# Value projections with the tokens stationary: 512 features wide in two half-depth chunks, in place of 256 features wide in two full-depth chunks

## The reference

```python
def token_mixing(u, w_in, ...):                       # mixer 0
    proj = u @ w_in
    gq, gk, gv, glr, gog, mq, mk, mv, ga, gb = jnp.split(proj, offsets, axis=-1)   # gv, mv: 512 wide each
    o_a = gla_chunked(heads(gq), heads(gk), heads(gv), heads(log_a))
    o_b = moba_attention(heads(mq), heads(mk), heads(mv), rel_bias)
    ...
for l in range(DEPTH_2):                              # mixers 1 and 2
    x = x + 0.5 * swiglu_2(rms_norm(x, ffn1_norm[l]), ffn1_w_in[l], ffn1_w_out[l])
    h = rms_norm(x, mix_norm[l]) @ w_mix_in[l]
    (c_x, c_b, c_c, h_q, h_f, h_i, h_g, f_q, f_k, f_v, f_f) = jnp.split(h, split_at, axis=-1)   # f_v: 512 wide
```

## Time and profile before

| | |
|---|---|
| median of 3 runs | 1642.5 us (1640.9 to 1642.66) |
| the profiled execution: span | 1640.7 us |
| TensorE busy | 1616.5 us (99%), 13617 records |
| VectorE busy | 1154.1 us (70%) |
| ScalarE busy | 799.1 us (49%) |
| GpSimd busy | 171.4 us (10%) |
| TensorE clock granted | 1.000 over the span |

### The profile page before, as it was taken

How to read it: one execution, slowest core, us unless ns; L and a number is a source line. 1 busy time by engine, 2 the same in 40 slices (tenths; PEclk the granted TensorE clock), 3 DMA queues, 4 the chain that set the end, 5 groups by cost and what they waited for, 6 DMA issues and landing times.

```text
span 1640.7 us, 33817 instructions
## 1 busy us (share of the span) xinstructions
PE 1616.5 (99%) x13617; PEld 1579.3 (96%) x13617; DVE 1154.1 (70%) x1452; ACT 799.1 (49%) x973; POOL 171.4 (10%) x193
## 2 busy tenths in 40 slices
PE   6999999999999999999999999999999999999999
PEld 4999999999999999999999999999999999999999
DVE  6877789778766657666688876656665588776653
ACT  3444445355544455444565654445444465554432
POOL 1100114500000000000052200000000035200000
PEclk9999999999999999999999999999999999999999
DMA  9998897646666467665744566568665764456653
GB/s 332 303 315 250 250 329 229 221 147 189 183 190 184 135 193 203 187 169 159 231 134 129 152 179 183 154 180 217 193 181 149 204 186 129 129 162 191 170 159 114
DMA packets 501553, 315.62 MB, mean 192 GB/s; under 512 B 14815, under 2 KB 489674, under 8 KB 501450
## 3 DMA queue, kind: packets, MB, share of 16 engines
q1 hardware_dynamic: 491824, 282.33, 60.5%
q0 software_dynamic: 8496, 29.92, 5.2%
q10 hardware_dynamic: 1130, 1.90, 0.3%
HBM read 313.04 MB, written 1.05 MB: 191 GB/s over the span
## 4 chain that ended last, share of the span: by engine, by line
PE 71%; DVE 4%; ACT 2%; issue 1%; ACTq 0%; DVEq 0%
PE accs L1747 20%; PE accs L1749 20%; PE accs L1748 19%; PE wide L1787 1%; PE accs L1787 1%; PE accs L1785 1%; PE wide L1785 1%; PE accs L1786 1%; PE wide L1786 1%; DVE wlo L1060 1%; PE wide L2018 1%; PE accs L1845 1%; PE accs L1847 0%; PE accs L1846 0%; PE ps_score L2067 0%
## 5 line engine op out<-in xcount | busy, mean ns | idle before, releaser
L1747 PE MATMUL accs<-uhi_shift,whi 128*128 128x256 f32 x2304 | 650.8, 282 | 3.0 <-DVE ulo L1111 1.2
L1749 PE MATMUL accs<-uhi_shift,wlo 128*128 128x256 f32 x2304 | 645.8, 280 | 0.0
L1748 PE MATMUL accs<-ulo,whi 128*128 128x256 f32 x2304 | 643.2, 279 | 0.0
L746 ACT CAST whi<-raw 128x2048 fp32r<-128x2048 f32 (+2 forms) x294 | 499.5, 1702 | 101.4 <-PE accs L1749 61.9
L1060 DVE TENSOR_TENSOR wlo<-raw,whi 128x2048 fp32r<-128x2048 f32 (+2 forms) x249 | 496.3, 2001 | 4.5 <-ACT gat L987 3.1
L1747 PEld LDWEIGHTS accs<-uhi_shift,whi 128*128 128x128 f32 x2304 | 433.4, 188 | 11.3 <-issue 5.2
L1748 PEld LDWEIGHTS accs<-ulo,whi 128*128 128x128 f32 x2304 | 434.3, 188 | 1.2 <-issue 1.2
L1749 PEld LDWEIGHTS accs<-uhi_shift,wlo 128*128 128x128 f32 x2304 | 433.2, 188 | 0.0
L1747 PE MATMUL accs<-hhi,whi 128*128 128x256 f32 x1056 | 297.6, 282 | 0.7 <-DVE wlo L1060 0.7
L1748 PE MATMUL accs<-hlo,whi 128*128 128x256 f32 x1056 | 298.0, 282 | 0.0
L1749 PE MATMUL accs<-hhi,wlo 128*128 128x256 f32 x1056 | 296.3, 281 | 0.0
(11 more groups left out here) (368 smaller groups left out, 2258.7 us busy)
## 6 DMA issues: line engine op xcount, KB each, us to landing
raw<-in_ffn_w_in SPq DMA_DIRECT2D x176, 512.0 KB, 5.1
in_turn<-in_w_ada POOLq DMA_DIRECT2D x56, 512.0 KB, 5.5
raw<-in_w_mix_in SPq DMA_DIRECT2D x52, 512.0 KB, 4.7
raw<-in_ffn_w_out SPq DMA_DIRECT2D x64, 384.0 KB, 3.6
raw<-in_w_ff_gate SPq DMA_DIRECT2D x44, 512.0 KB, 5.0
raw<-in_w_ff_up SPq DMA_DIRECT2D x44, 512.0 KB, 6.3
raw<-in_w_in SPq DMA_DIRECT2D x40, 512.0 KB, 5.0
raw<-in_ffn_w_out SPq DMA_DIRECT2D x64, 320.0 KB, 4.0
```

What stands on the lines that cost most here:

```text
L746: nc.scalar.copy(whi[:, n % RING, 0:cols], raw[:, n % RING, 0:cols]).then_inc(hi_ready, 1)
L1747: mm(dst, wh, xh, start=first, stop=False)
L1748: mm(dst, wh, xl, start=False, stop=False)
L1749: return mm(dst, wl, xh, start=False, stop=last)
```

## The change

The value chunks become pairs of a new kind "p". Both chunks of a pair cover the same 512 output columns; the first holds row tiles 0 to 3 (input features 0 to 511), the second row tiles 4 to 7. A chunk is now 2 token blocks x 4 row tiles x 3 = 24 products of 512 columns. Token block 0 accumulates in bank e % 2 over both chunks, token block 1 in bank (e+1) % 2. So the second bank is asked for in the middle of the first chunk, token block 0 is complete in the middle of the second (new counter `token_ready`), and VectorE evacuates it in the step of the second chunk. In mixers 1 and 2 chunk `av1` moves ahead of `g4`, so that the pair is adjacent; `lv0` there stays as it was.

```diff
-GLA_CHUNKS = [("lq", 0, "f"), ("lk", 256, "f"), ("lv0", 512, "t"), ("lv1", 768, "t"),
+GLA_CHUNKS = [("lq", 0, "f"), ("lk", 256, "f"), ("lv0", 512, "p"), ("lv1", 512, "p"),
...
-              ("av0", 2576, "t"), ("av1", 2832, "t"), ("g0", 1040, "f"), ("g2", 1296, "f")] + \
+              ("av0", 2576, "p"), ("av1", 2576, "p"), ("g0", 1040, "f"), ("g2", 1296, "f")] + \
...
-              ("ak0", 2304, "f"), ("ak1", 2560, "f"), ("av0", 2816, "t"), ("g4", 0, "f"), ("av1", 3072, "t"),
+              ("ak0", 2304, "f"), ("ak1", 2560, "f"), ("av0", 2816, "p"), ("av1", 2816, "p"), ("g4", 0, "f"),
...
+            def wide_rows(w, n, at, half_):
+                v = kview(raw, n % RING, KD // 2, 512)
+                src = w[half_ * D // 2:(half_ + 1) * D // 2, at:at + 512].rearrange("(k p) c -> p k c", p=P)
+                return [(v[:, 2 * j:2 * j + 2], src[:, 2 * j:2 * j + 2]) for j in range(2)]
...
+                if kind == "p":
+                    tt = int(name[2])
+                    if tt == 0:
+                        dve.wait_ge(token_ready, m + 1 + (m > 0 or name == "av0"))
+                    else:
+                        dve.wait_ge(chunk_used, RING + n0 + s + 1)
+                    v.tensor_scalar((lv if name[0] == "l" else av)[:, tt], acc[(e0 + s) % 2][:],
+                                    rstd[:, T + tt:T + tt + 1] if m else 1.0, None, ALU.mult).then_inc(evacuated, 1)
+                    return
                 dve.wait_ge(chunk_used, RING + n0 + s + 1)
...
                         if side == 0:
                             split_lo_half(n0 + s + LO_LEAD, 0)
+                            if second_half(m, s):
+                                take(m, s - 1)
...
-                    take(m, s)
+                    if not first_half_of_pair(m, s):
+                        take(m, s)
...
-            def third_of_in0(n, dst):
...
+            def token_half(n, e, half_, tt, waits=None):
+
+                d, c = acc[(e + tt) % 2], slice(tt * P, (tt + 1) * P)
+                if tt and not half_:
+                    bank_free(e + 1)
+                vh, vl = kview(whi, n % RING, KD // 2, 512), kview(wlo, n % RING, KD // 2, 512)
+                for i in range(KD // 2):
+                    k = half_ * KD // 2 + i
+                    if waits is not None and not tt:
+                        pe.wait_ge(ulo_ready, waits + k + 1)
+                    mm(d, uhi[:, k, c], vh[:, i], start=k == 0, stop=False)
+                    mm(d, uhi[:, k, c], vl[:, i], start=False, stop=False)
+                    ins = mm(d, ulo[:, k, c], vh[:, i], start=False, stop=k == KD - 1)
+                if half_ and not tt:
+                    ins.then_inc(token_ready, 1)
                 return ins
```

More of the change, by code:

```diff
@@ L333, in build @@
         evacuated = sem("evacuated")
+        token_ready = sem("token_ready")
         silu_ready = sem("silu_ready")
@@ L582, in mixer @@
                 n0 = FIRST[f"in{m}"]
-                for s, (_, at, _) in enumerate(IN_CHUNKS[m]):
-                    load(n0 + s, plain(in_w[m], n0 + s, at))
+                for s, (name, at, kind) in enumerate(IN_CHUNKS[m]):
+                    if kind == "p":
+                        load(n0 + s, wide_rows(in_w[m], n0 + s, at, int(name[2])))
+                    else:
+                        load(n0 + s, plain(in_w[m], n0 + s, at))
                     if m and s == GATES_BEHIND:
@@ L1481, in qk_norm, with first_half_of_pair, second_half @@
                 dve.sem_inc(aq_free, 1)
+            def first_half_of_pair(m, s):
+                return IN_CHUNKS[m][s][2] == "p" and IN_CHUNKS[m][s][0][2] == "0"
+            def second_half(m, s):
+                return IN_CHUNKS[m][s][2] == "p" and IN_CHUNKS[m][s][0][2] == "1"
             def take(m, s):
@@ L1824, in second_of_in0 @@
                         ins.then_inc(pe_z, 1)
-            def third_of_in0(n, dst):
-                waits = KD * SPLITS.index("in0u")
-                vh, vl = kview(whi, n % RING, KD, 256), kview(wlo, n % RING, KD, 256)
-                for k in range(KD):
-                    pe.wait_ge(ulo_ready, waits + k + 1)
-                    for tt in range(TT):
-                        c, d = slice(tt * P, (tt + 1) * P), dst[:, tt * 256:(tt + 1) * 256]
-                        mm(d, uhi[:, k, c], vh[:, k], start=k == 0 and tt == 0, stop=False)
-                        mm(d, uhi[:, k, c], vl[:, k], start=False, stop=False)
-                        ins = mm(d, ulo[:, k, c], vh[:, k], start=False, stop=k == KD - 1 and tt == 1)
+            def token_half(n, e, half_, tt, waits=None):
[12 more added lines that the diff above has]
+                    ins.then_inc(token_ready, 1)
                 return ins
@@ L2155, in mixer @@
                         second_of_in0(n0 + 1)
-                    elif m == 0 and s == 2:
-                        third_of_in0(n0 + 2, dst).then_inc(chunk_used, 1)
                     for side in range(2):
-                        if s < (1 if m else 3):
+                        if s < (1 if m else 2):
                             continue
-                        if IN_CHUNKS[m][s][2] == "t":
+                        if IN_CHUNKS[m][s][2] == "p":
+                            half_ = int(IN_CHUNKS[m][s][0][2])
+                            ins = token_half(n0 + s, e0 + s - half_, half_, side,
+                                             KD * SPLITS.index("in0u") if m == 0 and s < 4 else None)
+                        elif IN_CHUNKS[m][s][2] == "t":
                             ins = token_tiles(n0 + s, dst, [side])
```

4 lines of the change are left out of this document (3 added, 1 removed).

## The result

The changed kernel takes 1645.24 us (median of 16 runs, 1643.38 to 1650.42), the kernel before 1641.94 us in 16 runs beside them (1640.39 to 1643.24): a ratio of 1.0019, with an interval of 1.0013 to 1.0026. So it is 3.3 us slower. The interval leaves no doubt that it is slower, but the size is at the 0.2% that the prediction named as its bound for no change. The time is inside the stated range (1640.6 to 1645.8) and 2 us above the predicted 1643.2; as a change, +0.7 us was forecast and +3.3 came.

A forecast was written before the change was run, and what follows sets the result against it. TensorE, busy for 99% of the span, was taken to bound the kernel. Mixer 0's +1.65 us and -0.94 for mixers 1 and 2 made +0.7; on the 1642.5 median that gave 1643.2 us, range 1640.6 to 1645.8.

The forecast's parts named there:

- the price of a product: In eight value chunks, a 512-column product at 0.2155 us replaces two at 0.118, saving 3.8 us if nothing else moves.
- the ceiling of 0.2355: Upper bound in us on a 512-column product in the value chunks: twice the old price, nothing gained.
- rival 3: All value chunks: 512-column product costs twice the old, no gain anywhere; +2.35 to 3.15 us, 1644.9 to 1645.7; chance 0.08.
- The pair lv: Mixer 0, lv0 and lv1: waits for VectorE's evacuations make the chunk behind them start 2.35 us later, both chunks' saving lost.
- the middle wait of 2.9 us: Halfway through lv0 in mixer 0, TensorE waits from 258.6 to 261.5 for VectorE's evacuation of chunk 1.
- The pair av of mixer 0: Middle wait costs nothing; about 0.2 us of the first chunk and all 0.48 of the second gained, 0.7 together.
- Mixers 1 and 2: Their av pairs: VectorE's added evacuation leaves a lead of 0.47 us per mixer, about half the products' 0.96; 0.94 for both.
- the 0.52 us at 898.71: VectorE's idle time in mixer 1, from which its arrival at 898.24 instead of 898.71 was reckoned.
- the lead of 0.36 us: Mixers 1 and 2: time gained after av0, by which VectorE's step 7 was to start earlier with TensorE's key statistics.
- rival 1: All eight value chunks: full saving of 3.8 us arrives and the middle wait costs nothing, 1638.7 us; chance 0.08.
- rival 2: Clock falls in the new 2.9 us stall in lv0: 1648.8 if low over the pair's rest, 1644.4 if recovering; chance 0.15.
- The milder sum of rival 2: Clock recovers after some 6 us; the stall before chunk 4 swallows 2 of 3 us, giving 1644.4 us.

The follow-up runs named there:

- e5: Changed kernel without TensorE's wait for the second bank in the middle of lv0; 1646.96 us against 1642.15 for the kernel before, ratio 1.0028.
- e4_prices: Kernel before plus runs of 24 reduced-precision products of several widths behind its end, executed once; 512 columns 0.236 us each, 256 columns 0.119.
- e10_streams: Kernel before plus runs of 512-column products behind its end (plain, 64 rows, zeros, f32), executed once; plain 0.232 us each, zeros 0.236, f32 records 0.429.
- e6: e5 with VectorE's evacuation of the lv pair's first bank moved back to the step of lv0; 1642.41 us, ratio 1.0003 to the kernel before.
- e8: e6 with the wait for the second bank in the middle of lv0 kept; 1644.4 us against 1642.42 for the kernel before, ratio 1.0009.
- e9: e6 with the value chunks of mixers 1 and 2 as before the change; 1641.2 us against 1642.42 for the kernel before, ratio 0.9992.
- e1: Changed kernel with mixer 0's lv chunks as before the change, av pairs kept in all mixers; 1642.62 us against 1642.15 for the kernel before, ratio 1.0001.
- e3: Changed kernel with each 512-column product made as two of 256 columns; 1644.96 us, ratio 1.0014 to the kernel before.
- e2: Changed kernel with only mixer 0's lv chunks as a pair, av everywhere as before; 1644.15 us, ratio 1.0013 to the kernel before.

## Why the prediction came out as it did

**The step that failed: the price of a product**, "I take 0.2155: 0.020 us saved per new product, 0.48 us per chunk, 3.8 us for all eight". Measured are 0.232 in the changed kernel and 0.2335 over the whole of `lv0` in `e5` (5.37 us over 23 steps), in the middle 0.2325, and 0.229 to 0.236 alone (`e4_prices`, `e10_streams`). The saving is 2 x 0.118 - 0.2325 = 0.0035 us a product, 0.08 a chunk, 0.7 for all eight; a thousandth of a microsecond more or less in a price moves that by 0.2. The prediction reached its value from f32 records of the same streaming time, and had the ceiling of 0.2355 beside it; the truth lies next to the ceiling. The term was mis-sized by 3.1 us, of which 0.8 belong to the lv pair and lay under its waits in any case. What the page of the Trainium skill "TensorE: Matmul & The Clock Gate" (section "Wait — 56ns, not 53.3ns?") gave for the saving, 0.5 us in all, is near the 0.7 of the runs and far from my 3.8, although both of its prices are too low here (109 and 216 ns against 118 and 233).

That the time lies inside the range is in part luck. The kernel before measured 1641.94 us beside it, 0.56 less than the 1642.5 that the sum started from, and the range ends 0.56 above the measured time: on its own base the change would have come out at its very edge. The range reached that far because it was drawn to take in rival 3.

**The pair lv: +2.35 predicted, +2.71 measured.** The mechanism held in each piece: the middle wait of 2.9 us (3.04 from start to start, 2.8 beyond one product), the wait before `lv1` swallowed, the wait for the evacuation of `lv`, and, as said, hardly any dependence on the product's price. Of the 0.36 us that it was short, about 0.3 is VectorE's own sequence: the summing step took 1.63 us where the earlier trace rows and `e6` have 1.27, in the same place of the order. The traces show what differs: in the changed kernel it starts while an instruction of GpSimd is still going.

```profile
265.76 1.49 POOL L665 TENSOR_TENSOR work<-bcum 128x256 f32<-128x256 f32 x1
```

That is until 267.25, and the summing step started at 266.71. In `e6` the same instruction takes 0.60 us and is over at 267.83, 1 us ahead of the summing step. `e6` and `e8` show what the prediction did not separate: with an early evacuation the middle wait costs some 1.0, without one both together cost 2.7.

**The pair av of mixer 0: -0.7 predicted, -0.17 measured.** That is 48 x 0.0035. Nothing waits, neither at the middle nor, contrary to the prediction, at the block sums. First the timeline of VectorE and GpSimd in the kernel before, then that of VectorE and TensorE in the changed one:

```profile
298.40 1.75 DVE L1236 SCALAR_TENSOR_TENSOR gat<-in_turn,c_act,gat 128x1024 f32<-128x1024 f32 x1
299.03 1.59 POOL L660 TENSOR_TENSOR work<-bcum 128x256 f32<-128x256 f32 x1
```

```profile
296.39 0.69 DVE L1542 TENSOR_SCALAR ak<-accs 128x512 f32<-128x512 f32 x1 [1.61 <-PE accs L1776]
299.24 1.28 DVE L1245 SCALAR_TENSOR_TENSOR gat<-in_turn,c_act,gat 128x1024 f32<-128x1024 f32 x1
...
301.96 1.22 DVE L1258 TENSOR_REDUCE in_block<-gat 128x32 f32<-128x1024 f32 x1
304.14 0.25 PE L1928 MATMUL bank<-in_block,quadrants 128*32 128x8 f32 x8
```

VectorE is done at 303.18, nearly 1 us ahead of TensorE. It needs 6.79 us from the evacuation of `ak1` on, where the prediction took the 7.57 of the trace before: its low part takes 1.22 instead of 1.50 and its summing step 1.28 instead of 1.75. In the trace before both overlap instructions of GpSimd (297.36 to 300.62), in the changed one neither does. So even a saving of 0.48 us a chunk would have met no wait there (7.84 - 0.48 is above 6.79), and the 0.7 was too small for its own price.

**Mixers 1 and 2: -0.47 each predicted, +0.38 and +0.50 measured.** The products give 0.17 us. The added evacuation costs time on VectorE, as foreseen, but TensorE meets it earlier than the prediction looked. The changed kernel's timeline of VectorE in mixer 1, for the earlier trace rows:

```profile
868.93 1.65 DVE L1078 TENSOR_TENSOR wlo<-raw,whi 128x1024 fp32r<-128x1024 f32 x1
870.50 0.74 DVE L1510 TENSOR_SCALAR av<-accs,rstd 128x512 f32<-128x512 f32 x1
871.16 0.28 DVE L1447 TENSOR_REDUCE st_max<-ps_score 128x1 f32<-128x128 f32 x1
```

And its timeline of TensorE: the start of the pair, of the chunk behind it, and the softmax transposes of the step after that.

```profile
855.01 0.50 PE L1863 MATMUL accs<-whi,uhi_shift 128*128 128x512 f32 x1
...
871.38 0.36 PE L1774 MATMUL accs<-uhi_shift,whi 128*128 128x256 f32 x1
...
884.07 0.41 PE L2104 MATMUL bank<-causal_r,ident_r 128*128 128x128 f32 x1
884.64 0.52 PE L2114 MATMUL ps_turn<-const,prob 128*128 128x128 f32 x3 [0.17 <-ACT gat L878]
```

The chunk behind the pair starts 16.37 us after it; in the earlier trace rows it is 870.31 - 853.99 = 16.32. So the wait for the evacuation, some 0.2 us, ate the 0.17 of the products. The evacuation stands ahead of the first softmax and pushes it 0.6 us back (from 15.56 to 16.15 us behind the pair's start). Nearly half of that is won back in the softmax, whose third instruction took 0.50 us beside GpSimd before and takes 0.17 now. The other 0.33 us pass on through ScalarE to the transposes, which come 0.57 us after the scores (884.07 to 884.64), against 0.27 in the trace before. They are never given back. In mixer 2 the same distances are 16.44 against 16.32 and again 0.3 at the transposes, which makes most of the +0.50.

That nothing was spare there can be seen in the trace before:

```profile
870.19 0.50 DVE L1440 TENSOR_SCALAR st_max<-st_max 128x2 f32<-128x2 f32 x1
...
882.67 0.47 ACT L869 COPY gat<-ps_turn 128x384 f32<-128x384 f32 x1
883.29 0.52 PE L2083 MATMUL ps_turn<-const,prob 128*128 128x128 f32 x3
```

ScalarE's copy ends 0.15 us ahead of the transposes (883.14), as it does in the changed kernel (884.50). So here a second step of the prediction failed: it took VectorE's slack to be the 0.52 us at 898.71, but TensorE depends on the same chain at 883.29, where the slack is nil. Even with the lead of 0.36 us that it gave VectorE there, the chain would have been no earlier than before (an estimate: +0.6 for the evacuation, -0.3 in the softmax, -0.36), and the mixers would have gained nothing.

**The sum.** Predicted +0.7, in the trace +3.46. The difference of 2.8 is 0.36 at the pair lv, 0.53 at the pair av of mixer 0 and 1.8 in mixers 1 and 2. The 0.53 is the price. Of the 1.8 some 0.9 is the slack that was looked for in the wrong place (2 x 0.47), and most of the rest the price, through the lost lead. So rival 3 was right, a product of 512 columns at twice the old, and not the forecast that stood first. It said +2.35 to +3.15 us; the runs have +3.3, the trace +3.46.

**The other rivals.** The full saving (rival 1) is out: there was none to arrive. Of rival 2, the clock, the mechanism exists: after a wait of 3.2 us in `e5` and of 3.0 us in `e8` the granted clock went to the half level and came back. The same page of the Trainium skill (section "What's actually happening") says that idleness halves the clock and sustained work restores it, and these two traces agree; a fall without such a wait stands in the last section. (The milder sum of rival 2 has a slip of 0.2: 1643.2 and the 1 us that isn't swallowed make 1644.2.) But the clock does not explain the result: the profiled execution of the changed kernel has its clock at 1.00 in every stretch of the pair and is +3.46 us all the same. Of its 16 runs nine had a mean clock of 0.998 or less; their median was 1645.4, that of the seven at 1.000 was 1644.5. So it may add half a microsecond to the median. But a lower mean clock doesn't say that it fell at the pair: the traces of `e4`, `e8` and `e9` have stretches at the half level near 42 and 209 us, that of `e1` one near 209 and that of `e10` one near 248, all ahead of `lv0`. And the eleven runs of `e3`, with the same waits, all have a mean clock of 0.999 or more and a median of 1644.96. So this part is not settled.

## What to carry to other kernels

Price a product of another shape from products of the same number format; if there is none in the trace, a term that carries the whole forecast deserves the pessimistic bound, or the case nearer to it as the forecast. Wider products save only what a product costs beyond its columns, 3 ns of 118 here; they pay only where they cost nothing else. When work is accumulated across two chunks, look at the step in which its bank is given back and at every counter that it passes on the way: the bank was free for microseconds here, the counter wasn't. Removing one of two waits on the same late engine merges them, and the longer one can cost the clock as well. And before a lead is carried past another engine, look for the first place at which the two meet, not for the place where the idle time is easiest to see; and ask whether that engine's instructions were slowed by a third one that will have moved.

## What was not expected of the hardware

A reduced-precision product with a stationary block of 128 x 128 costs 0.118 to 0.119 us at 256 columns, 0.176 at 384 and 0.229 to 0.236 at 512: about 0.45 ns a column and 3 ns, at a granted clock of 1.00. An f32 record costs 0.429 at 512 and 0.215 at 256, which is 0.84 ns a column. So the reduced-precision product is 7 to 10% dearer than half an f32 record. Half the stationary width, half the rows, and zeros as data change it by no more than 3%.

An instruction of VectorE can take longer beside one of GpSimd. The summing step of 128x1024 takes 1.27 to 1.29 us in 44 of its 49 places in the trace before, and 1.75 to 1.76 in the five in which GpSimd has a TENSOR_TENSOR going; in the changed kernel the two that overlap one take 1.63 and 1.64. GpSimd pays too: L675 takes 1.77 us beside the summing step at 272.98, and 0.73 for the same work at 296.66, where none runs. That it is the overlap that makes it was not tested by a run of its own.

A wait of TensorE of about 3 us in an otherwise dense stretch can be followed by a stretch at the half clock or not: it was after 3.2 us in `e5` and 3.0 us in `e8`, and wasn't after the same 3.0 us in the profiled executions of the changed kernel, of `e2` and of `e3`. Nor does it take a long wait. In `e9`, whose longest wait in the 25 us before was 0.47 us, the clock fell behind 16 products of one column (206.20 to 208.15), in which TensorE is busy by its records but streams one column at a time, and 1.5 us of products of 256 columns. Its stretches (columns as above):

```profile
205.00:209.50 4.50, 4.03 (x35) 3.83 (x34) 4.08 (x5) 1.74 (x2) 0.66 (x2) 1.00 1.07 315
209.50:212.90 3.40, 3.40 (x19) 3.40 (x18) 0.00 (x0) 0.00 (x0) 0.40 (x1) 0.50 1.02 327
```

The same products at the same place left the clock at 1.00 in the traces of the kernel before and the changed one. What decides was not found.
